# Gated delta rule in a hybrid decoder block: state times keys before the inverse, one application of the inverse

## The chip, the cores and the metric

The kernel runs on one core of one Trainium2 chip. The metric is device time in microseconds (us), the median of several runs. The engines: TensorE (PE in the rows; PEld is its weight load), VectorE (DVE), ScalarE (ACT), GpSimd (POOL) and SyncE (SP), which issues the weight loads.

## What is computed

One decoder block over 16 meta tokens and 256 tokens, width 1024, all in float32: RMS norm, one input projection, differential attention, in parallel a gated delta rule (8 heads of 128), both merged through gates, an output projection, then a mixture of 32 experts. The diff is in the delta rule. The reference computes it in chunks of tokens:

```python
T = triangular_solve(A + eye, eye)                    # the inverse of each chunk
u = einsum('bhnij,bhnje->bhnie', T, v * beta[..., None])
w = einsum('bhnij,bhnjd->bhnid', T, kb * jnp.exp(gc)[..., None])     # kb = k * beta
def step(S, inp):
    v_new = u_n - einsum('bhcd,bhde->bhce', w_n, S)
    o_n = einsum('bhcd,bhde->bhce', qd_n, S) + einsum('bhij,bhje->bhie', qk_n, v_new)
    S = S * gt_n[..., None, None] + einsum('bhcd,bhce->bhde', kd_n, v_new)
    return S, o_n
```

So v_new = T(v·beta) - (T(k·beta·e^gc))S, which is the same as T(v·beta - (k·beta·e^gc)S).

## The kernel before

The kernel takes the meta tokens as a first small chunk and then two chunks (rounds) of 128 tokens, t=0 and t=1. The eight heads are two groups of four, c=0 and c=1, each with eight work buffers `w[0]` to `w[7]` of [128, 4, 128] and three PSUM banks X, Y and Z. The state `S` is [128, 8, 128]. Each round is a chain of named steps, listed in `STEPS`:

- s0 makes the decay matrix and K·K', s1 and s2 turn it and make Q·K'; s3 to s6 build the inverse of 16-wide blocks, x1, t1, x2, t2, x3, t3 join them to 32, 64 and 128 (small 64x64 products). `w[0]` ends as the transposed inverse.
- s7 turns the keys on PE; DVE makes `w[7]` = keys x kdec and `w[2]` = keys x begc (beta·e^gc) from it. POOL masks for x1.
- x3 ends with a small DVE product, t3 with a DVE copy into `w[0]` and `w[4]` = v·beta.
- w multiplies `w[2]` with the inverse, and ACT copies it with scale -1 to `w[6]`.
- v makes v_new in Z from two products per head, `w[0]`·`w[4]` and `w[6]`·S; ACT copies it to `w[5]`.
- o makes the output and the update of S, q the sum of squares for the norm.

A step runs on PE first, then on those of DVE, ACT and POOL that `WORKS` names for it. Semaphores per group and engine (`dn_pe`, `dn_dve`, `dn_act`, `dn_pool`) count the steps; PE's part of a step waits until the other engines have done all earlier steps of its group (`wait_step(..., before=True)`), and the others wait for PE's part of the step. `link` adds a wait for the instruction's own completion, `mark` counts it without the wait.

The order on PE is written out in `MIX_ORDER`. It goes through groups of entries: ten single steps of the meta chunk, then each step of a round for c=0 and c=1. 26 projection tiles (gate2 to gate7, ga0 to ga7, ya0 to ya7, gb0 to gb3) are spread over them by this rule:

```python
while given < len(filler) and given * (len(groups) - 4) < i * len(filler):
    MIX_ORDER.append(("tile", filler[given]))
```

With 18 steps there are 46 groups. PE's order around the rounds comes out as (a step stands for both head groups): [meta s7] [meta w] gate7 [meta m] ga0 [s0] [s1] ga1 [s2] ga2 [s3] [s4] ga3 [s5] [s6] ga4 [s7] ga5 [x1] [t1] ga6 [x2] [t2] ga7 [x3] ya0 [t3] [w] ya1 [v] ya2 [o] [q] ya3 for t=0, and for t=1 [s0] [s1] ya4 [s2] ya5 [s3] [s4] ya6 [s5] ya7 [s6] [s7] gb0 [x1] [t1] gb1 [x2] gb2 [t2] [x3] gb3 [t3] [w] [v] [o] [q]. DVE, ACT and POOL follow `BEHIND`: the same order, except that what they do with a tile's result comes after the next step of c=0. A gate or gb tile is 24 products with operands split in a high and a low part (L740); ACT and DVE split each tile's weights three tiles ahead (L278, L283). A ya tile is eight float32 products (L722).

Lines of the steps: s7 PE L938 to L942, DVE L1733 and L1737, POOL L654; x1, x2 PE L943 (helper L909), ACT L1346; t1 DVE L1740, L1741; x3 PE L951, DVE L1750; t3 PE L954, DVE L1752, L1753; w PE L959 (helper L887), ACT L1348; v PE L967, L968, ACT L1350.

Of the kernel before, what the change touches and what calls it, by code (L numbers as in the profile page):

```python
# [13 lines left out]
P = 128  # L14
D = 1024
NC = D // P
Q = P // 2
# [23 lines left out]
ALU = mybir.AluOpType  # L41
# [23 lines left out]
def hybrid_block(nc, x, meta_tokens, norm1_w, w_in, lambda_q1, lambda_k1, lambda_q2, lambda_k2, da_subln_w,  # L65
# [3 lines left out]
    with ExitStack() as ctx:  # L69
# [278 lines left out]
        TR_NO = {k: i for i, k in enumerate(TR)}  # L348


        STEPS = ["s0", "s1", "s2", "s3", "s4", "s5", "s6", "s7", "x1", "t1", "x2", "t2", "x3", "t3", "w", "v", "o", "q"]
        META_STEPS = ["s0", "s1", "s2", "s3", "s4", "s5", "s6", "s7", "w", "m"]

        DN = [("meta", 0, s) for s in META_STEPS]
        for t in range(TT):
# [2 lines left out]
        WORKS = {  # L358
            "pe": set(STEPS + META_STEPS),
            "dve": {"s0", "s1", "s2", "s3", "s4", "s5", "s6", "s7", "t1", "t2", "x3", "t3", "q", "m"},  # L360
            "act": {"s0", "s2", "s3", "s4", "s5", "s7", "x1", "x2", "w", "v", "o", "q", "m"},
            "pool": {"s1", "s7", "t1", "q"},
        }

# [8 lines left out]
        def works(engine, key):  # L373
            t, _, s = key
            if t == "meta":
                if engine == "pool":
                    return False
                if engine in ("dve", "act") and s == "w":
                    return engine == "dve"
            if engine == "dve" and s == "o":  # L380
                return t == 0
            return s in WORKS[engine]
# [299 lines left out]
        def _(pe):  # L682
# [190 lines left out]
            def dn(t, c, s):  # L873
                w = work[c]
                X, Y, Z = (bank[2 + 3 * c + i][:, :].rearrange("p (h i) -> p h i", h=4) for i in range(3))
                n = 1 if t == "meta" else 4

                for engine in ("act", "dve", "pool"):
                    wait_step(pe, engine, (t, c, s), before=True)
                if (t, c, s) == DN[0]:  # L880
                    pe.wait_ge(tr_copied, len(TR))
                    pe.wait_ge(qk_ready, N_DN)
                    pe.wait_ge(gate_cols, 2)

                def each(o, lhsT, rhs, start=True, stop=True):
                    for h in range(n):
                        last = pe.matmul(o[:, h, :], lhsT(h), rhs(h), start=start, stop=stop)  # L887
                    return last

                if t == "meta":  # L890
                    kT = lambda h: dkT_meta.rearrange("p h i -> p (h i)")
                    vT = lambda h: dvT_meta.rearrange("p h i -> p (h i)")
                    col = lambda h: g[:, 2 * H:2 * H + 1]
                    lower = tri16
                else:
                    cols = slice(META + t * P, META + (t + 1) * P)
                    kT = lambda h: dkT[:, 4 * c + h, cols]
                    qT = lambda h: dqT[:, 4 * c + h, cols]
                    col = lambda h: g[:, t * H + 4 * c + h:t * H + 4 * c + h + 1]
                    lower = tri  # L900
                buf = lambda i: (lambda h: w[i][:, h, :])
                Xs, Ys, Zs = (bank[2 + 3 * c + i][:, 0:4 * Q].rearrange("p (h i) -> p h i", h=4) for i in range(3))

                def both(o, lhsT, rhs, quarters=(0, 1)):

                    for h in range(n):
                        for q in quarters:
                            rows = slice(q * Q, (q + 1) * Q)
                            last = pe.matmul(o[rows, h, :], lhsT[rows, h, :], rhs[rows, h, :], start=True, stop=True,  # L909
                                             tile_position=(q * Q, q * Q))  # L910
                    return last

                T, TT_, X_ = small(c, 6, 0), small(c, 5, 1), small(c, 5, 0)
                if s == "s0":
                    each(X, lambda h: col(h).broadcast_to([P, P]), lambda h: lower)
                    last = each(Y, kT, kT)
                elif s == "s1":
                    for h in range(n):
                        last = pe.transpose(X[:, h, :], w[1][:, h, :], ident)
                    if t != "meta":  # L920
                        last = each(Z, kT, qT)
                elif s == "s2":
                    for h in range(n):
                        last = pe.transpose(Y[:, h, :], w[2][:, h, :], ident)
                elif s == "s3":
                    both(Xs, small(c, 4, 0), small(c, 4, 1))
                    last = both(Zs, small(c, 4, 1), small(c, 4, 0))
                elif s == "s4":
                    both(Ys, small(c, 5, 0), T)
                    both(Xs, small(c, 5, 1), small(c, 5, 0))  # L930
                    last = both(Zs, small(c, 5, 0), small(c, 5, 1))
                elif s == "s5":
                    both(Ys, small(c, 4, 0), T)
                    last = both(Xs, small(c, 4, 1), small(c, 4, 0))
                elif s == "s6":
                    last = both(Zs, small(c, 5, 0), T)
                elif s == "s7":
                    both(Xs, T, ident_c.unsqueeze(1).broadcast_to([P, 4, Q]))  # L938
                    for h in range(n):
                        last = pe.transpose(Y[:, h, :], kT(h), ident)  # L940
                    if t == "meta":
                        last = pe.transpose(Z[:, 0, :], vT(0), ident)  # L942
                elif s in ("x1", "x2"):  # L943
                    last = both(Zs, small(c, 4, 0), T)
                elif s in ("t1", "t2"):
                    both(Xs, X_, TT_)

                    last = both(Zs, TT_, X_, (0, 1) if s == "t1" else (0,))
                elif s == "x3":
                    for h in range(n):  # L950
                        last = pe.matmul(Zs[Q:P, h, :], w[1][0:Q, h, Q:P], T[0:Q, h, :], start=True, stop=True, tile_position=(0, Q))  # L951
                elif s == "t3":
                    for h in range(n):
                        last = pe.matmul(Xs[0:Q, h, :], X_[Q:P, h, :], w[0][Q:P, h, Q:P], start=True, stop=True, tile_position=(Q, 0))  # L954
                elif s == "w":
                    if t == "meta":
                        last = pe.matmul(Z[:, 0, :], w[0][:, 0, :], w[3][:, 0, :], start=True, stop=True)
                    else:
                        last = each(X, buf(2), buf(0))  # L959
                elif s == "m":  # L960

                    for half in range(2):
                        last = pe.matmul(bank[2 + half][:, :], w[7][:, 0, :], um[:, 4 * half:4 * half + 4, :],
                                         start=True, stop=True)
                elif s == "v":
                    for h in range(n):
                        pe.matmul(Z[:, h, :], w[0][:, h, :], w[4][:, h, :], start=True, stop=False)  # L967
                        last = pe.matmul(Z[:, h, :], w[6][:, h, :], S[:, 4 * c + h, :], start=False, stop=True)  # L968
                elif s == "o":
                    for h in range(n):  # L970
                        pe.matmul(Y[:, h, :], S[:, 4 * c + h, :], qT(h), start=True, stop=False)
                        last = pe.matmul(Y[:, h, :], w[5][:, h, :], w[3][:, h, :], start=False, stop=True)
                    if t < TT - 1:
                        last = each(X, buf(7), buf(5))
                elif s == "q":
                    last = pe.matmul(Z, ones, w[6], start=True, stop=True)
                last.then_inc(dn_pe[c], 1)
# [162 lines left out]
        def _(act):  # L1140
# [175 lines left out]
            def dn(t, c, s):  # L1316
# [27 lines left out]
                    last = act.activation(small(c, 5, 1)[:, 0:n, :], Xs[:, 0:n, :], ACT.Copy)  # L1344
                elif s in ("x1", "x2"):
                    last = act.activation(small(c, 5, 0)[:, 0:n, :], Zs[:, 0:n, :], ACT.Copy)  # L1346
                elif s == "w" and t != "meta":
                    last = act.activation(w[6][:, 0:n, :], X[:, 0:n, :], ACT.Copy, scale=-1.0)  # L1348
                elif s == "v":
                    last = act.activation(w[5][:, 0:n, :], Z[:, 0:n, :], ACT.Copy)  # L1350
                elif s == "m":
# [99 lines left out]
        def _(dve):  # L1451
# [233 lines left out]
            def dn(t, c, s):  # L1685
# [46 lines left out]
                elif s == "s7":  # L1732
# [1 line left out]
                    if t == "meta":  # L1734
                        last = tt(b(3), Z, per_head(beta), ALU.mult)
                    else:
                        last = tt(b(2), Y, per_head(begc), ALU.mult)  # L1737
                elif s == "t1":
                    turned = small(c, 5, 1)[:, 0:n, :]
                    tt(turned, Xs, turned, ALU.add)  # L1740
# [6 lines left out]
                        last = tt(diagonal(b(0), q), Xs[rows], small(c, 5, 1)[rows, 0:n, :], ALU.add)  # L1747
                elif s == "x3":

                    last = tt(small(c, 5, 0)[Q:P], Zs[Q:P], per_head(nbeta)[Q:P, :, 0:Q], ALU.mult)  # L1750
                elif s == "t3":
                    dve.tensor_copy(b(0)[0:Q, :, Q:P], Xs[0:Q])  # L1752
                    last = tt(b(4), dv_tok[:, t, hs, :], per_head(beta), ALU.mult)  # L1753
                elif s == "w":

                    last = tt(um, Z[:, 0, :].unsqueeze(1).broadcast_to([P, H, P]),
# [193 lines left out]
```

## Time and profile before

| | |
|---|---|
| median of 3 runs | 745.88 us (745.85 to 747.65) |
| profiled execution | 743.06 us, its span 741.3 us |
| mean granted TensorE clock | 0.943 |
| PE busy | 628.2 us, 85% of the span |
| DVE busy | 322.0 us, 43% |
| ACT busy | 247.1 us, 33% |
| POOL busy | 46.1 us, 6% |
| chain that ended last | PE 67%, DMA 16%, DVE 7%, ACT 4% |

The profile is of one execution. A busy share is the union of an engine's instructions; matmuls are pipelined, so PE's issue times tell more than their ends. The chain of work that ended last follows each step back to what released it. The rounds of the delta rule stand between 264 and 420 us.

### The profile page before, as it was taken

Reading aid. Unit: us, or ns where it says so; the run is one execution under the profiler, and the core shown is the slowest. Engines: PE = TensorE matmul, PEld = TensorE weight load, DVE = VectorE, ACT = ScalarE, POOL = GpSimd, SP = SyncE. Lnnn points to the kernel's source line nnn. Section 1 sums busy time; section 2 is a strip of 40 time slices with the busy share of each in tenths; the row PEclk is TensorE's granted clock in tenths of the full one; section 3 lists DMA queues with packets and bytes.
Section 4 is the critical chain, followed back from the end, with each engine's and each line's share of the span. In section 5 each row is a group of like instructions: output and inputs, shape, how many; then the busy total and the mean of one; then the engine's idle time right before and its main releaser. Section 6 shows DMA issues by size and latency. Waiting matters only on the chain.

```text
span 741.3 us, 12849 instructions
## 1 busy us (share of the span) xinstructions
PE 628.2 (85%) x5127; PEld 498.3 (67%) x5127; DVE 322.0 (43%) x717; ACT 247.1 (33%) x548; POOL 46.1 (6%) x94
## 2 busy tenths in 40 slices
PE   2899999899999979999898999976896686867954
PEld 2899998789988879987788898854333323413321
DVE  4534349899878647522634273143210110201103
ACT  5335547667674434313222550121110110101102
POOL 8000000000000001201111100020000000000000
PEclk9989999999999989999999999997999988978988
DMA  9845443323334411111143077960899999999991
GB/s 292 252 137 167 157 153 114 105 70 112 114 114 132 153 57 59 59 57 57 52 132 104 2 260 262 423 255 1 346 422 422 422 422 422 422 422 423 421 385 57
DMA packets 69686, 156.40 MB, mean 211 GB/s; under 512 B 7042, under 2 KB 56308, under 8 KB 57348
## 3 DMA queue, kind: packets, MB, share of 16 engines
q1 hardware_dynamic: 65792, 154.36, 55.5%
q10 hardware_dynamic: 3844, 1.34, 0.7%
q8 instruction: 35, 0.57, 0.3%
q14 instruction: 15, 0.12, 0.0%
HBM read 154.64 MB, written 1.05 MB: 210 GB/s over the span
## 4 chain that ended last, share of the span: by engine, by line
PE 67%; DMA 16%; DVE 7%; ACT 4%; issue 3%; SPq 1%; POOL 1%; DVEq 0%; ACTq 0%; POOLq 0%
PE bank L740 29%; DMA arena<-in_expert_w_up_dram 15%; PE bank L1069 9%; PE bank L909 4%; PE bank L722 4%; PE bank L729 4%; PE bank L887 2%; PE bank L851 1%; PE bank L828 1%; PE bank L1088 1%; PE bank L1057 1%; SPq L481 1%; PE bank L1095 1%; PE bank L796 1%; DVE w_lo L283 1%
## 5 line engine op out<-in xcount | busy, mean ns | idle before, releaser
L740 PE MATMUL bank<-uT_hi,w_hi 128*128 128x272 f32 (+1 forms) x576 | 175.7, 305 | 5.7 <-issue 4.2
L740 PE MATMUL bank<-uT_lo,w_hi 128*128 128x272 f32 (+1 forms) x576 | 166.7, 289 | 0.0
L740 PE MATMUL bank<-uT_hi,w_lo 128*128 128x272 f32 (+1 forms) x576 | 166.5, 289 | 0.0
L283 DVE TENSOR_TENSOR w_lo<-arena,w_hi 128x1024 fp32r<-128x1024 f32 x80 | 98.6, 1235 | 48.3 <-ACT w_hi L278 48.0
L740 PEld LDWEIGHTS bank<-uT_hi,w_hi 128*128 128x128 f32 x576 | 111.4, 193 | 8.5 <-issue 6.8
L740 PEld LDWEIGHTS bank<-uT_lo,w_hi 128*128 128x128 f32 x576 | 111.5, 194 | 1.5 <-issue 0.5
L740 PEld LDWEIGHTS bank<-uT_hi,w_lo 128*128 128x128 f32 x576 | 111.3, 193 | 0.0
L1069 PE MATMUL bank<-arena 128*32 128x512 f32 x512 | 68.8, 698 | 42.3 <-DMA arena<-in_expert_w_up_dram 39.1
L278 ACT ACTIVATE w_hi<-arena 128x1024 fp32r<-128x1024 f32 x80 | 83.8, 1052 | 4.5 <-PE bank L740 4.2
L1069 PEld LDWEIGHTS bank<-arena 128*32 128x32 f32 x512 | 19.7, 126 | 85.7 <-issue 85.7
L1875 DVE COPY arena<-bank 128x256 f32<-128x256 f32 x8 | 3.4, 425 | 108.6 <-PE bank L1076 108.6
L1423 ACT ACTIVATE arena<-bank 128x256 f32<-128x256 f32 x8 | 3.1, 384 | 120.9 <-PE bank L1069 120.9
L1578 DVE SCALAR_TENSOR_TENSOR arena<-arena 128x272 f32<-128x272 f32 x72 | 37.8, 525 | 7.5 <-ACT arena L1210 5.8
L1088 PE MATMUL bank<-arena 128*32 128x512 f32 x256 | 34.0, 679 | 4.1 <-DVE arena L1882 4.1
L909 PE MATMUL bank<-arena 64*64 64x64 f32 x964 | 34.2, 220 | 1.5 <-ACT arena L1346 0.8
L909 PEld LDWEIGHTS bank<-arena 64*64 64x64 f32 x964 | 31.1, 134 | 5.8 <-issue 1.5
L1057 PEld LDWEIGHTS bank<-arena 128*128 128x128 f32 x256 | 31.1, 199 | 3.3 <-issue 3.3
L1057 PE MATMUL bank<-arena 128*128 128x128 f32 x256 | 31.2, 282 | 0.0
L1095 PE MATMUL bank<-arena 128*128 128x512 f32 x64 | 29.6, 605 | 0.0
L729 PE MATMUL bank<-arena 128*128 128x256 f32 x128 | 28.7, 380 | 1.1 <-DVE arena L1653 1.1
L722 PE MATMUL bank<-arena 128*128 128x256 f32 x128 | 29.3, 382 | 0.0
L729 PEld LDWEIGHTS bank<-arena 128*128 128x128 f32 x128 | 24.0, 190 | 4.3 <-issue 1.2
(319 smaller groups left out, 867.6 us busy)
## 6 DMA issues: line engine op xcount, KB each, us to landing
arena<-in_w_in_dram SPq DMA_DIRECT2D x36, 1024.0 KB, 5.2
arena<-in_expert_w_gate_dram SPq DMA_DIRECT2D x32, 1024.0 KB, 16.7
arena<-in_expert_w_up_dram SPq DMA_DIRECT2D x32, 1024.0 KB, 18.5
arena<-in_expert_w_down_dram SPq DMA_DIRECT2D x32, 1024.0 KB, 17.6
arena<-in_w_branch_attn_dram SPq DMA_DIRECT2D x4, 1024.0 KB, 5.0
arena<-in_w_branch_dn_dram SPq DMA_DIRECT2D x4, 1024.0 KB, 5.2
arena<-in_w_out_dram SPq DMA_DIRECT2D x4, 1024.0 KB, 5.1
arena<-in_x_dram SPq DMA_DIRECT2D x4, 512.0 KB, 5.0
```

The costliest lines, as they stand in the source:

```text
L278: nc.scalar.activation(w_hi[q % NSPLIT], split_source(nc.scalar, q), ACT.Copy).then_inc(w_hi_ready, 1)
L283: nc.vector.tensor_tensor(w_lo[q % NSPLIT], src, w_hi[q % NSPLIT].bitcast(F32), ALU.subtract).then_inc(w_lo_ready, 1)
L722: last = pe.matmul(ps[:, 0:SEQ], unit(u)[:, c, half * P:(half + 1) * P], yaT[:, c, :], start=(c == 0), stop=(c == NC - 1))
L729: last = pe.matmul(ps[:, 0:SEQ], mixT[:, c, t * P:(t + 1) * P], unit(u)[:, c, :], start=(c == 0), stop=(c == NC - 1))
L740: last = pe.matmul(ps[:, 0:b.shape[2]], a[:, c, :], b[:, c, :], start=(c == 0 and i == 0), stop=(c == NC - 1 and i == 2))
L887: last = pe.matmul(o[:, h, :], lhsT(h), rhs(h), start=start, stop=stop)
L909: last = pe.matmul(o[rows, h, :], lhsT[rows, h, :], rhs[rows, h, :], start=True, stop=True, tile_position=(q * Q, q * Q))
L1057: last = pe.matmul(bank[6 + group][:, (c % 4) * P:(c % 4 + 1) * P], u2[:, t, c * P:(c + 1) * P], pick[:, t].rearrange("p e s -> p (e s)"), ...
L1069: last = pe.matmul(bank[4][CAP * e:CAP * (e + 1), :], xg[:, c, CAP * e:CAP * (e + 1)], gate_up(e, odd)[:, c], start=(c == 0), stop=(c == N ...
L1088: last = pe.matmul(bank[6 + half][CAP * e:CAP * (e + 1), :], hidT[:, fc, CAP * e:CAP * (e + 1)], down_of(e)[:, fc, half * 512:(half + 1) * ...
L1095: last = pe.matmul(bank[2 * t + half][:, :], pickT[:, t, :], dsb[:, half * 512:(half + 1) * 512], start=False, stop=False, skip_group_chec ...
L1578: last = stt(a, x_[:, k:k + L], tap(k, c), a, ALU.mult, ALU.add)
```

## The change

The step w leaves the rounds (the meta chunk keeps its own). In s7 PE also multiplies the state onto the keys, K·S, into Z, and DVE scales that by begc into `w[2]`. In x3 DVE makes, behind the small product (which signals at once), v·beta in `w[4]` and `w[4]` - `w[2]` in `w[2]`. v is one product per head, `w[0]`·`w[2]`. With 17 steps the rule above has 44 groups, so the tiles fall elsewhere between the steps: [meta s7] gate7 [meta w] [meta m] ga0 [s0] ga1 [s1] [s2] ga2 [s3] ga3 [s4] [s5] ga4 [s6] ga5 [s7] [x1] ga6 [t1] [x2] ga7 [t2] ya0 [x3] [t3] ya1 [v] ya2 [o] [q] ya3, and for t=1 [s0] ya4 [s1] [s2] ya5 [s3] ya6 [s4] [s5] ya7 [s6] gb0 [s7] [x1] gb1 [t1] gb2 [x2] [t2] gb3 [x3] [t3] [v] [o] [q].

```diff
--- before.py
+++ after.py
@@ -348,7 +348,7 @@
         TR_NO = {k: i for i, k in enumerate(TR)}
 
 
-        STEPS = ["s0", "s1", "s2", "s3", "s4", "s5", "s6", "s7", "x1", "t1", "x2", "t2", "x3", "t3", "w", "v", "o", "q"]
+        STEPS = ["s0", "s1", "s2", "s3", "s4", "s5", "s6", "s7", "x1", "t1", "x2", "t2", "x3", "t3", "v", "o", "q"]
         META_STEPS = ["s0", "s1", "s2", "s3", "s4", "s5", "s6", "s7", "w", "m"]
 
         DN = [("meta", 0, s) for s in META_STEPS]
@@ -358,7 +358,7 @@
         WORKS = {
             "pe": set(STEPS + META_STEPS),
             "dve": {"s0", "s1", "s2", "s3", "s4", "s5", "s6", "s7", "t1", "t2", "x3", "t3", "q", "m"},
-            "act": {"s0", "s2", "s3", "s4", "s5", "s7", "x1", "x2", "w", "v", "o", "q", "m"},
+            "act": {"s0", "s2", "s3", "s4", "s5", "s7", "x1", "x2", "v", "o", "q", "m"},
             "pool": {"s1", "s7", "t1", "q"},
         }
 
@@ -375,8 +375,8 @@
             if t == "meta":
                 if engine == "pool":
                     return False
-                if engine in ("dve", "act") and s == "w":
-                    return engine == "dve"
+                if engine == "dve" and s == "w":
+                    return True
             if engine == "dve" and s == "o":
                 return t == 0
             return s in WORKS[engine]
@@ -940,6 +940,9 @@
                         last = pe.transpose(Y[:, h, :], kT(h), ident)
                     if t == "meta":
                         last = pe.transpose(Z[:, 0, :], vT(0), ident)
+                    else:
+
+                        last = each(Z, kT, lambda h: S[:, 4 * c + h, :])
                 elif s in ("x1", "x2"):
                     last = both(Zs, small(c, 4, 0), T)
                 elif s in ("t1", "t2"):
@@ -953,19 +956,14 @@
                     for h in range(n):
                         last = pe.matmul(Xs[0:Q, h, :], X_[Q:P, h, :], w[0][Q:P, h, Q:P], start=True, stop=True, tile_position=(Q, 0))
                 elif s == "w":
-                    if t == "meta":
-                        last = pe.matmul(Z[:, 0, :], w[0][:, 0, :], w[3][:, 0, :], start=True, stop=True)
-                    else:
-                        last = each(X, buf(2), buf(0))
+                    last = pe.matmul(Z[:, 0, :], w[0][:, 0, :], w[3][:, 0, :], start=True, stop=True)
                 elif s == "m":
 
                     for half in range(2):
                         last = pe.matmul(bank[2 + half][:, :], w[7][:, 0, :], um[:, 4 * half:4 * half + 4, :],
                                          start=True, stop=True)
                 elif s == "v":
-                    for h in range(n):
-                        pe.matmul(Z[:, h, :], w[0][:, h, :], w[4][:, h, :], start=True, stop=False)
-                        last = pe.matmul(Z[:, h, :], w[6][:, h, :], S[:, 4 * c + h, :], start=False, stop=True)
+                    last = each(Z, buf(0), buf(2))
                 elif s == "o":
                     for h in range(n):
                         pe.matmul(Y[:, h, :], S[:, 4 * c + h, :], qT(h), start=True, stop=False)
@@ -1344,8 +1342,6 @@
                     last = act.activation(small(c, 5, 1)[:, 0:n, :], Xs[:, 0:n, :], ACT.Copy)
                 elif s in ("x1", "x2"):
                     last = act.activation(small(c, 5, 0)[:, 0:n, :], Zs[:, 0:n, :], ACT.Copy)
-                elif s == "w" and t != "meta":
-                    last = act.activation(w[6][:, 0:n, :], X[:, 0:n, :], ACT.Copy, scale=-1.0)
                 elif s == "v":
                     last = act.activation(w[5][:, 0:n, :], Z[:, 0:n, :], ACT.Copy)
                 elif s == "m":
@@ -1734,7 +1730,8 @@
                     if t == "meta":
                         last = tt(b(3), Z, per_head(beta), ALU.mult)
                     else:
-                        last = tt(b(2), Y, per_head(begc), ALU.mult)
+
+                        last = tt(b(2), Z, per_head(begc), ALU.mult)
                 elif s == "t1":
                     turned = small(c, 5, 1)[:, 0:n, :]
                     tt(turned, Xs, turned, ALU.add)
@@ -1747,10 +1744,12 @@
                         last = tt(diagonal(b(0), q), Xs[rows], small(c, 5, 1)[rows, 0:n, :], ALU.add)
                 elif s == "x3":
 
-                    last = tt(small(c, 5, 0)[Q:P], Zs[Q:P], per_head(nbeta)[Q:P, :, 0:Q], ALU.mult)
+                    tt(small(c, 5, 0)[Q:P], Zs[Q:P], per_head(nbeta)[Q:P, :, 0:Q], ALU.mult).then_inc(dn_dve[c], 1)
+                    link(tt(b(4), dv_tok[:, t, hs, :], per_head(beta), ALU.mult))
+                    mark(tt(b(2), b(4), b(2), ALU.subtract))
+                    return
                 elif s == "t3":
-                    dve.tensor_copy(b(0)[0:Q, :, Q:P], Xs[0:Q])
-                    last = tt(b(4), dv_tok[:, t, hs, :], per_head(beta), ALU.mult)
+                    last = dve.tensor_copy(b(0)[0:Q, :, Q:P], Xs[0:Q])
                 elif s == "w":
 
                     last = tt(um, Z[:, 0, :].unsqueeze(1).broadcast_to([P, H, P]),
```

## Rows read from the trace of the kernel before

**Rows 1.** The chain that ended last, at the start of the expert stage: start us, us, what

```profile
545.97 18.34 DMA arena<-in_expert_w_up_dram
```

**Rows 2.** Windows: four stretches of the rounds, two stretches of lower clock

```profile
core 0: us, PE busy (x) PEld busy (x) DVE busy (x) ACT busy (x) POOL busy (x), PEclk, DMA share, GB/s
264.27:281.42 17.15, 12.97 (x90) 12.34 (x89) 10.33 (x15) 5.47 (x14) 3.38 (x2) 0.80 0.19 61
270.49:277.31 6.82, 5.44 (x25) 5.17 (x26) 3.14 (x5) 2.71 (x6) 1.28 (x1) 0.50 0.00 0
281.42:332.16 50.74, 49.68 (x731) 46.50 (x730) 25.35 (x52) 14.89 (x31) 4.68 (x4) 1.00 0.18 56
346.87:362.94 16.07, 11.02 (x81) 10.23 (x81) 9.02 (x14) 3.75 (x11) 3.67 (x3) 1.00 0.21 65
362.94:415.12 52.18, 49.26 (x699) 45.16 (x698) 22.09 (x47) 13.96 (x28) 4.85 (x4) 0.97 0.31 102
403.60:407.02 3.42, 3.42 (x18) 3.42 (x17) 1.23 (x2) 0.00 (x0) 0.00 (x0) 0.50 0.00 0
```

**Rows 3.** Waits of PE, 242 to 428 us: total us, times, longest

```profile
PE bank L919 <- issue: 5.1, 2, 2.7
PE bank L919 <- DVE arena L1709: 3.8, 2, 2.4
```

**Rows 4.** Timeline of PE around v at t=0: start us, us, what

```profile
328.59 0.38 PE L967 MATMUL bank<-arena 128*128 128x128 f32 x2
332.16 0.38 PE L722 MATMUL bank<-arena 128*128 128x256 f32 x1
```

**Rows 5.** Timeline of x3, t3 and w at t=0

```profile
316.97 0.43 DVE L1750 TENSOR_TENSOR arena<-bank,arena 64x256 f32<-64x256 f32 x1 [0.91 <-PE bank L951]
...
321.69 0.42 DVE L1752 COPY arena<-bank 64x256 f32<-64x256 f32 x1 [3.51 <-PE bank L954]
322.12 0.69 DVE L1753 TENSOR_TENSOR arena<-arena 128x512 f32<-128x512 f32 x1
...
322.92 2.38 PE L887 MATMUL bank<-arena 128*128 128x128 f32 x16 [0.80 <-issue]
```

**Rows 6.** Timeline of the meta chunk's w and m

```profile
256.58 0.46 PE L957 MATMUL bank<-arena 128*128 128x128 f32 x2 [0.21 <-DVE arena L1735]
...
257.84 1.22 DVE L1756 TENSOR_TENSOR arena<-bank,arena 128x1024 f32<-128x1024 f32 x1
...
259.72 1.88 PE L963 MATMUL bank<-arena 128*128 128x512 f32 x4
```

**Rows 7.** Timeline: s1 of group 1 at t=0; a table load at t=1

```profile
274.50 1.09 PE L919 MATMUL bank<-arena 128*128 128x128 f32 x4 [1.38 <-DVE arena L1709]
...
388.24 1.28 ACT L1217 ACT_TABLE_LOAD   x1
```

**Rows 8.** Timeline behind s7 at t=0

```profile
299.91 0.69 DVE L1733 TENSOR_TENSOR arena<-bank,arena 128x512 f32<-128x512 f32 x1 [2.68 <-PE bank L940]
300.52 0.68 DVE L1737 TENSOR_TENSOR arena<-bank,arena 128x512 f32<-128x512 f32 x1
301.37 0.74 POOL L654 TENSOR_TENSOR arena<-arena 128x256 f32<-128x256 f32 x1 [20.47 <-DVE arena L1737]
302.57 1.23 DVE L283 TENSOR_TENSOR w_lo<-arena,w_hi 128x1024 fp32r<-128x1024 f32 x1
302.76 1.62 POOL L654 TENSOR_TENSOR arena<-arena 128x256 f32<-128x256 f32 x1 [0.65 <-DVE arena L1737]
```

**Rows 9.** Windows: s3-s4, s7, x2-t2 at t=0; x1-t1, t2-x3 at t=1

```profile
284.45:289.26 4.81, 4.81 (x161) 4.74 (x160) 2.73 (x6) 1.43 (x4) 0.00 (x0) 1.00 0.54 171
298.60:300.82 2.22, 2.22 (x41) 1.92 (x41) 0.91 (x2) 0.66 (x2) 0.00 (x0) 1.00 0.94 306
310.05:313.22 3.17, 3.15 (x82) 2.95 (x81) 1.11 (x4) 1.88 (x4) 0.00 (x0) 1.00 0.03 8
387.11:391.32 4.21, 3.38 (x97) 3.07 (x96) 0.96 (x3) 3.27 (x5) 0.78 (x2) 1.00 0.93 303
398.48:403.07 4.59, 3.30 (x66) 3.01 (x65) 2.98 (x8) 1.33 (x2) 0.00 (x0) 1.00 0.67 228
```

## The prediction, made before the changed kernel was run

> **What bounds the kernel now.** I looked first at the page's busy shares and its chain of work that ended last, to see who sets the pace (TensorE, PE in the rows), then at the stage of the delta rule, 255 to 420 us, the only one that the diff touches. What leaves that stage comes out at the end: behind it the chain runs on PE through the projections and the router into the first expert batch, and only from 546 us does it stand on expert weights, whose loads are issued once a batch of experts has used its slots [rows 1]. So a microsecond won or lost before 420 us moves the end by about one.
>
> Inside the stage I measured four stretches by windows: round t=0 from s0 to the end of s2, then to the end of v; the same for t=1 [rows 2]. In the long ones PE is busy for 49.68 of 50.74 and 49.26 of 52.18 us: mostly the tiles and products themselves set the pace. In the short ones it is busy for 12.97 of 17.15 and 11.02 of 16.07 us, and the waits say why: s1 waits for VectorE's (DVE) masked decay, 5.1 and 3.8 us over four waits [rows 3]. The granted clock stands at 0.50 from 270.49 to 277.31 and from 403.60 to 407.02 us, and at 1.00 elsewhere in the stage [rows 2].
>
> **Part 1, work on PE.** One 128x128x128 product costs 0.223 us: v issues 16 of them from 328.59 to 332.16 [rows 4]. The four products of w per head group become the four of K·S in s7, an even trade. v falls from eight to four per group: 16 fewer in all, 16 x 0.223 = 3.6 us off PE, 1.8 a round.
>
> **Part 2, the step w goes.** At t=0, t3's second half has issued by 322.05, and w starts at 322.92, behind the DVE copy and the product with beta [rows 5]; its second half waits again. The wait of some 0.8 us and the second of 0.25 go: 1.1; at t=1 0.9 by the same reading. ScalarE's copy with scale -1 goes too, hidden now behind ya1 at t=0 and the other group at t=1, so worth nothing.
>
> **Part 3, DVE work that moves.** x3 now has the small product, v·beta and the subtraction, 0.69 us for each large one (the subtraction is priced as the product, both 128x512 from SBUF) [rows 5]. t3 needs only the first, but DVE takes its queue in order: group 1's small product stands behind group 0's two large ones and a tile's output.
>
> **Part 4, the order written out for PE.** This is the part that speaks against the change. With 17 steps the 26 tiles fall between other pairs of steps. Worked out by the formula of the order, the new neighbours without a tile between are w-m (start), then at t=0 s1-s2, s4-s5, s7-x1, t1-x2, x3-t3, and at t=1 s1-s2, s4-s5, s7-x1, x2-t2, x3-t3-v. No longer neighbours are s0-s1, s3-s4, s5-s6 (s6-s7 at t=1), x1-t1, t3-w, and x2-t2 at t=0, t2-x3 at t=1. The costs, each followed through the queues:
>
> *w-m at the start.* m waits for DVE's 1.22 us spread of w's result; gate7 covered it, w at 256.58 and m at 259.72 [rows 6]. Without the cover w to m takes about 1.7 us instead of 0.2, and the 0.2 to 0.5 us that w itself waits is now covered: +1.1.
>
> *s0 to s2.* s1's second half can't start before DVE's decay of group 1, 274.4 at t=0 [rows 7], with ga1 before it or not. Behind it remain s1 (1.35 us at full clock), DVE's two products and GpSimd's q product (POOL, 1.3), now with no tile over them, while the tile's 2.9 us fill the first wait. t=0: 17.15 to 16.1, -1.1. t=1: 16.07 to 15.3, -0.8.
>
> *s7-x1.* s7 takes 2.22 us for both groups now, 1.1 to 1.2 each [rows 9], and 0.89 more per group for K·S: 2.1. x1 waits for POOL's product, which waits for both DVE products of s7. From s7's start: group 0's DVE 2.2 to 3.5, POOL to 4.4 (0.74 alone), x1 at 4.55 where PE was free at 4.2; group 1's PE part ends at 4.2, DVE 4.35 to 5.6, POOL to 6.5, x1 at 6.7 where PE was free at 5.1. Idle 0.35 + 1.6 = 1.95 us at t=0; at t=1 ScalarE's table load of 1.28 us [rows 7] falls between its two copies and holds gb0's output on DVE before group 1: 2.35. Before, a tile stood there and covered all of it.
>
> *t1-x2 at t=0.* DVE 0.75 for two 128x256 operations, POOL 0.74 [rows 8] and three handovers of 0.15 make 1.9 us, against 0.96 for the other group's t1: idle 1.0 + 0.45.
>
> *x3-t3.* The first small product ends 1.15 us after x3's start [rows 5]. v·beta, the subtraction and the tile's output then fill DVE to 2.7, group 1's small product to 3.15; t3's second half starts at 3.25 where PE was free at 1.8: 1.6 with the first gap, in each round. At t=1 v follows at once, and waits until the t3 copy at 4.85 where PE was free at 3.8: 1.1.
>
> The waits that go are read from pairs of steps that had no tile between: a 64x64 product costs 0.060 us (80 in 4.81) [rows 9], so x2-t2 at t=0, 40 of them, waited 3.17 - 2.4 = 0.8 us; x1-t1 at t=1, 48, waited 4.21 - 2.9 = 1.3; t2-x3 at t=1, 24 and eight of 0.13, 4.59 - 2.5 = 2.1 [rows 9]. For s5-s6, s6-s7 and x1-t1 at t=0 I estimate 0.3 each in the same way.
>
> Sums at full clock. t=0, ga2 to v: 50.74 - 1.8 (work) - 2.5 (w 1.1, x1-t1 0.3, x2-t2 0.8, s5-s6 0.3) + 5.15 (1.95, 1.45, 1.6, s4-s5 0.15) + 0.4 (more tiles start behind small products, 3.65 against 3.46 for a ya tile) = 52.0, **+1.3**. t=1, ya5 to v: 52.18 - 1.8 - 4.6 (w 0.9, x1-t1 1.3, t2-x3 2.1, s6-s7 0.3) - 1.7 (gb3 takes 4.55 us at clock 0.50, others 2.85) + 6.0 (2.35, x2-t2 0.8, 1.6, 1.1, s4-s5 0.15) + 0.2 = 50.3, **-1.9**. With the start +1.1 and the two short stretches -1.9 the whole is **-1.4 us**: the 3.6 us of saved work and 2 us around w are mostly spent on new waits.
>
> **The clock.** That sum has no stretch at 0.50. Before there are two: one came behind a 2.4 us wait, the other behind short gaps amid the small products of t2 and x3; yet s0-s1 at t=1, with as long waits, kept 1.00 [rows 2, 3]. The first cost about 1.1 (s1's second half in 2.45 instead of 1.35), the second 1.7. The new order has more places of that kind (s7-x1 twice, x3-t3 twice, s1-s2 twice), but a fall that meets an idle PE costs little. I take two falls at 1.1: +2.2. Bounds: none, 0; four, +4.4. Sum -1.4 + 2.2 = **+0.8**. The profiled execution took 743.06 (span 741.3), the median of the three runs is 745.88; I put the difference on the median: **746.7**.
>
> The Trainium skill ("TensorE: Matmul & The Clock Gate", HAM oscillation) says that gaps in the matmul stream bring the array back to half rate and that the next products start cold. The trace agrees at 270.49 and not at t=1, as above; by that rule alone each of the six new gaps would count, which is the second rival.
>
> POOL's product took 0.74 us alone and 1.62 us beside DVE's split at 302.57 [rows 8]; I price it at 0.74 in s7-x1, since the next split there waits for ScalarE, behind x1's copies. If it were 1.62 there, +0.9 a round. The Trainium skill ("SBUF — State Buffer") calls the pair of ports an exclusive lock; the row agrees: POOL ends 0.58 us after the split.
>
> **The rivals.** *The waits don't come, PE's saved work does.* If s7-x1 costs nothing (POOL's and DVE's work for group 1 done in time), 4.3 us less: 742.4. For it: PE is over 95% busy in the long stretches, so these steps have mostly been covered. Against: s7 signals once, at its end, and 2.5 us of DVE, POOL and handovers stand between it and x1 of the same group. It decides from 3 us less waiting than I count. Chance 0.26.
>
> *The clock falls at most of the new gaps.* One mechanism: PE's activity thins around s7-x1 and x3-t3, the clock goes to 0.50, and tiles or v and o behind it run at half rate, 1.7 us as gb3 did. With four falls at about 1.3 us: -1.4 + 5.2 = +3.8, 749.7; slower by over 0.3% from the third full one. For it: the fall at 403.60 came after gaps of under 1 us. Against: t=1 s0-s1. Chance 0.26.
>
> The forecast, gaps and savings about even, has 0.48, with its own range 744.2 to 748.1.
>
> **How the numbers follow.** 0.3% is 2.2 us, about what a measurement of this kernel tells from no change. Faster is the first rival (0.25, the rest of it within), slower the second (0.27 with a little of the forecast's edge), same 0.48. The range reaches into both: 742.0 (two falls fewer, or most of s7-x1 hidden) to 749.5 (four falls).
>
> **What would show it.** x1 behind s7 waiting for POOL, about 2 us in each round; t3's second half waiting for DVE's small product by 1.5 us; m behind DVE's spread; v in 1.8 us for both groups; s0-s1 without its first wait; stretches at 0.50, where and how many. It would be wrong if s7-x1 shows under 1 us of waits, or if the projections and the first expert batch don't shift along with the stage.

## The result and the profile after

The changed kernel takes 752.25 us (median of four, 751.39 to 754.74) against 745.87 before: ratio 1.0113, interval [1.0065, 1.0161]. It is slower by about 1.1%. Forecast was 746.7, no change, in a range up to 749.5. The profiled execution took 751.41 us (span 749.6, 8.3 more than before), mean granted clock 0.934.

First the windows of the kernel after: the four stretches of [rows 2] (s0 to s2 and ga2 to v at t=0, s0 to s2 and ya5 to v at t=1), then every stretch of the stage at clock 0.50.

```profile
core 0: us, PE busy (x) PEld busy (x) DVE busy (x) ACT busy (x) POOL busy (x), PEclk, DMA share, GB/s
264.43:280.59 16.16, 11.37 (x90) 10.57 (x89) 10.53 (x18) 5.76 (x15) 2.56 (x2) 0.86 0.20 65
280.59:336.49 55.90, 51.24 (x715) 47.31 (x713) 25.95 (x51) 13.74 (x27) 2.90 (x4) 0.95 0.14 40
351.20:366.50 15.30, 11.21 (x81) 10.21 (x81) 9.21 (x15) 4.27 (x12) 3.64 (x3) 1.00 0.22 70
366.50:420.52 54.02, 49.28 (x682) 45.13 (x681) 23.34 (x49) 12.34 (x24) 3.75 (x4) 0.93 0.31 99
275.93:282.75 6.82, 4.35 (x21) 3.72 (x20) 6.31 (x13) 2.49 (x5) 2.56 (x2) 0.50 0.00 0
330.54:333.95 3.41, 3.41 (x10) 2.70 (x9) 0.47 (x2) 0.00 (x0) 0.00 (x0) 0.50 0.00 0
395.39:398.80 3.41, 3.41 (x27) 3.29 (x28) 0.91 (x1) 1.33 (x2) 0.00 (x0) 0.50 0.04 11
415.87:422.70 6.83, 5.72 (x27) 5.75 (x28) 1.30 (x3) 1.20 (x2) 0.00 (x0) 0.50 0.01 2
```

The short stretches shrank, from 17.15 and 16.07 to 16.16 and 15.30 us. The long ones grew, from 50.74 and 52.18 to 55.90 and 54.02, though PE has 32 records fewer on the page (5095 against 5127). And the stage has four falls of the clock where [rows 2] has two, two of them (6.8 us) twice as long as the others. The rest of the 8.3 us: +1.2 from the meta chunk's w and m, -1.0 ahead of it, 1.05 in o and q at t=1 (the last third of that last fall lies there), and 1.8 behind the stage.

The waits of PE, 242 to 428 us (total, times, longest), and what stands behind s7 at t=0:

```profile
PE bank L924 <- POOL arena L651: 4.8, 4, 2.1
PE bank L909 <- POOL arena L654: 4.8, 6, 1.6
PE bank L957 <- issue: 3.2, 2, 1.7
PE bank L919 <- DVE arena L1705: 2.3, 1, 2.3
PE bank L919 <- issue: 1.8, 1, 1.8
PE bank L963 <- DVE arena L1755: 1.4, 1, 1.4
PE bank L887 <- issue: 1.3, 1, 1.3
```

```profile
306.07 0.69 DVE L1729 TENSOR_TENSOR arena<-bank,arena 128x512 f32<-128x512 f32 x1 [0.60 <-PE bank L887]
306.31 0.68 PE L909 MATMUL bank<-arena 64*64 64x64 f32 x16 [0.28 <-POOL arena L654]
306.68 0.68 DVE L1734 TENSOR_TENSOR arena<-bank,arena 128x512 f32<-128x512 f32 x1
...
307.53 0.72 POOL L654 TENSOR_TENSOR arena<-arena 128x256 f32<-128x256 f32 x1 [1.37 <-DVE arena L1734]
308.40 0.68 PE L909 MATMUL bank<-arena 64*64 64x64 f32 x16 [1.41 <-POOL arena L654]
```

x1 of both groups waits for GpSimd's product, which waits for both of VectorE's; in [rows 8] a tile lay over the same chain. Next, x3 and t3 at t=0:

```profile
325.99 0.43 DVE L1747 TENSOR_TENSOR arena<-bank,arena 64x256 f32<-64x256 f32 x1 [2.45 <-PE bank L954]
326.45 0.69 DVE L1748 TENSOR_TENSOR arena<-arena 128x512 f32<-128x512 f32 x1
...
327.17 0.69 DVE L1749 TENSOR_TENSOR arena<-arena 128x512 f32<-128x512 f32 x1
327.90 0.42 DVE L1646 TENSOR_TENSOR arena<-bank,arena 128x256 f32<-128x256 f32 x1
328.35 0.43 DVE L1747 TENSOR_TENSOR arena<-bank,arena 64x256 f32<-64x256 f32 x1
...
328.88 0.65 PE L957 MATMUL bank<-arena 64*64 64x64 f32 x8 [1.72 <-issue]
```

The reader sees DVE's queue in its order: group 0's small product, v·beta (L1748), the subtraction (L1749), a tile's output, and only then group 1's small product, for which t3's second half has waited 1.72 us. And t2 of both groups, which stands by itself between two tiles here, takes 2.01 us from its first product to the tile behind it:

```profile
319.62 2.08 PE L909 MATMUL bank<-arena 64*64 64x64 f32 x48
321.63 3.72 PE L722 MATMUL bank<-arena 128*128 128x256 f32 x16
```

Behind the stage the shift passes on whole: from the first product of gb4 to the first of the expert stage it is 86.88 us in both profiles (420.10 to 506.98, and 426.55 to 513.43). Then the first gather runs 6.01 us instead of 4.87, at the lower clock, and the chain reaches the weights 1.2 us later still:

```profile
513.43 6.01 PE bank L1055 x32
...
553.65 18.24 DMA arena<-in_expert_w_up_dram
```

### The profile page after: what moved, and what is told of

Same layout as the page of the kernel before. It is cut to its first block, busy times and chain, and to the rows that moved or that the text cites. A ratio compares the mean times of both kernels' runs of the same rounds, so it can differ in the third digit from the quotient of the medians.

```text
span 749.6 us, 12781 instructions
## 1 busy us (share of the span) xinstructions
PE 629.5 (84%) x5095; PEld 499.8 (67%) x5095; DVE 325.0 (43%) x721; ACT 245.0 (33%) x544; POOL 45.8 (6%) x94
## 3 DMA queue, kind: packets, MB, share of 16 engines
HBM read 154.64 MB, written 1.05 MB: 208 GB/s over the span
## 4 chain that ended last, share of the span: by engine, by line
PE 66%; DMA 16%; DVE 8%; ACT 4%; issue 4%; SPq 1%; POOL 1%; DVEq 0%; POOLq 0%; ACTq 0%
PE bank L740 29%; DMA arena<-in_expert_w_up_dram 15%; PE bank L1067 9%; PE bank L909 4%; PE bank L729 4%; PE bank L722 4%; PE bank L887 2%; PE bank L851 2%; PE bank L828 1%; PE bank L1055 1%; PE bank L1086 1%; SPq L481 1%; PE bank L1093 1%; DVE w_lo L283 1%; PE bank L796 1%
## 5 line engine op out<-in xcount | busy, mean ns | idle before, releaser
L1055 PEld LDWEIGHTS bank<-arena 128*128 128x128 f32 x256 | 32.2, 205 | 3.3 <-issue 3.3
L722 PE MATMUL bank<-arena 128*128 128x256 f32 x128 | 31.0, 398 | 0.0
L729 PE MATMUL bank<-arena 128*128 128x256 f32 x128 | 28.7, 380 | 1.1 <-DVE arena L1649 1.1
L722 PEld LDWEIGHTS bank<-arena 128*128 128x128 f32 x128 | 24.9, 199 | 4.1 <-issue 0.5
```

Source lines behind the costliest of these rows:

```text
L722: last = pe.matmul(ps[:, 0:SEQ], unit(u)[:, c, half * P:(half + 1) * P], yaT[:, c, :], start=(c == 0), stop=(c == NC - 1))
L729: last = pe.matmul(ps[:, 0:SEQ], mixT[:, c, t * P:(t + 1) * P], unit(u)[:, c, :], start=(c == 0), stop=(c == NC - 1))
L1055: last = pe.matmul(bank[6 + group][:, (c % 4) * P:(c % 4 + 1) * P], u2[:, t, c * P:(c + 1) * P], pick[:, t].rearrange("p e s -> p (e s)"), ...
```

## The experiments

My theory after the result: the algebra itself saves time, the places that the tiles got cost more than it saves, partly in waits and partly in falls of the clock that follow them. The rival: the algebra costs, through K·S in s7 and the longer DVE part of x3.

**The changed kernel again.** 

> The changed kernel again, unaltered, with more executions: how far its time scatters and how that goes with the granted clock. Expected: median 751 to 753, executions over 5 us apart, the slower ones at the lower mean clock.

Measured: 753.02 us (750.46 to 753.27, six executions), ratio 1.0094 [1.0058, 1.0131]. The scatter is under 3 us, less than I expected, and the slower ones don't show the lower mean clock (752.69 at 0.925, 753.23 at 0.936). Its profile (span 751.5) repeats the first one: the same four stretches to 0.06 us and the same four falls, all some 0.4 us later. The kernel before scatters more: of 23 further executions of it, those at a mean clock of 0.943 to 0.945 took 740.0 to 743.2 us, those at 0.933 took 742.2 to 748.0.

**Old places, new algebra.**

`spots` counts the missing w of each round again, so that each tile falls between the same steps as in the kernel before.

```diff
+        spots = [i + (i >= 24) + (i >= 41) for i in range(len(groups))]
...
-            while given < len(filler) and given * (len(groups) - 4) < i * len(filler):
+            while given < len(filler) and given * 42 < spots[i] * len(filler):
```

> The changed algebra (17 steps) with all 26 tiles between the same steps as before. Theory (the loss is where the tiles fall, and the clock behind the new gaps): s7-x1, t1-x2 and x3-t3 have a tile between again; 3.6 us of PE work and the waits of w are gone; span 5 to 6 us under that of before, about 736, median about 740. Rival (the algebra itself costs: K times S in s7 and the longer DVE part of x3 sit on the path): still over before, about 750.

Measured: 734.12 us (733.52 to 739.47), ratio 0.9843 [0.9804, 0.9882]. Its windows, the same four stretches and then its falls:

```profile
263.49:280.66 17.17, 12.40 (x91) 11.84 (x89) 10.35 (x15) 5.01 (x13) 3.40 (x2) 0.80 0.19 61
280.66:328.40 47.74, 47.60 (x715) 44.64 (x714) 27.55 (x54) 14.05 (x30) 3.79 (x4) 1.00 0.16 47
343.12:359.20 16.08, 12.28 (x82) 11.39 (x81) 9.02 (x14) 3.76 (x11) 3.66 (x3) 0.89 0.21 66
359.20:410.23 51.03, 48.70 (x683) 44.64 (x681) 24.26 (x49) 12.77 (x26) 3.78 (x4) 0.93 0.32 105
270.78:277.61 6.83, 4.45 (x23) 4.18 (x22) 3.64 (x6) 2.29 (x6) 1.28 (x1) 0.50 0.00 0
349.29:352.70 3.41, 2.76 (x12) 2.47 (x12) 1.50 (x3) 1.76 (x5) 0.00 (x0) 0.50 0.00 0
400.49:407.32 6.83, 6.79 (x35) 6.48 (x36) 4.61 (x7) 0.26 (x1) 0.00 (x0) 0.50 0.05 15
```

The short stretches are those of before to 0.02 us. The long one at t=0 is 3.0 us shorter than before and PE is busy for 47.60 of 47.74 us: 1.8 us of products and 1.1 us of waits around w are gone, and nothing has taken their place. The rival falls: with the tiles in their old places the algebra is a gain of about 11 us by the medians. This profile was one of its two slowest executions (739.42), so its span shows less.

**New places, old algebra.**

Here `spots` leaves w out of the count, and no tile may fall ahead of w.

```diff
+        spots = [i - (i > 24) - (i > 42) for i in range(len(groups))]
...
-            while given < len(filler) and given * (len(groups) - 4) < i * len(filler):
+            while given < len(filler) and given * 40 < spots[i] * len(filler) and i not in (24, 42):
```

> The algebra of before (18 steps) with the tiles between the steps where the changed kernel has them, w directly behind t3. Theory (placement): slower than before by about as much as the change, +5 to +9 us, since 3.6 us of products stay and w's waits too, but DVE's queue at x3 is short. Rival (algebra): within 2 us of before.

Measured: 748.39 us (746.30 to 753.15), ratio 1.0047 [1.0018, 1.0077]; the profiled execution, at 750.52, one of the slower. By the medians that is 3 us slower, less than expected:

```profile
263.74:279.90 16.16, 11.66 (x90) 10.86 (x89) 10.53 (x18) 5.76 (x15) 2.56 (x2) 0.85 0.19 65
279.90:336.67 56.77, 52.84 (x731) 49.29 (x730) 24.38 (x49) 14.93 (x29) 2.90 (x4) 0.95 0.16 50
351.38:366.69 15.31, 11.21 (x82) 10.22 (x82) 9.21 (x15) 4.28 (x12) 3.64 (x3) 1.00 0.22 68
366.69:421.39 54.70, 51.14 (x699) 46.46 (x697) 21.95 (x47) 13.43 (x26) 3.74 (x4) 0.94 0.30 98
```

The short stretches are those of the changed kernel to 0.01 us. The long ones are 6.0 and 2.5 us over before, and there are four falls too, at 274.93 (6.8 us), 326.13, 367.09 and 397.81 (3.4 us each). So in this profile the places cost the old algebra 6.8 us of the stage, and the stage is as long as in the changed kernel (162.63 us from s0 to gb4, against 162.12): what the new algebra saves is lost again. By the medians the places cost the old algebra 3 us and the new one 18. The waits show one thing that the new algebra adds here. The new x3 puts 1.4 us more per group in DVE's queue just where these places leave x3 and t3 side by side, and t3 waits 3.2 us in all, against 0.3 with the old algebra. What else sets the medians apart, one profile of each doesn't say.

**Gaps filled.** Products of `ident` and `tri` that nothing reads, into a PSUM bank that is free at that time.

```diff
+                def keep_busy(k):
+                    for i in range(k):
+                        pe.matmul(bank[3][:, (i % 4) * P:(i % 4 + 1) * P], ident, tri, start=True, stop=True)
...
+                if t != "meta":
+                    keep_busy({("s1", 0): 9, ("s1", 1): 8, ("x1", 0): 6, ("x3", 1): 0, ("t3", 0): 7}.get((s, c), 0))
+                    if t == 1 and (s, c) == ("t3", 1):
+                        keep_busy(4)
```

> The changed kernel with extra products into a free PSUM bank in the gaps behind s1, x1 and t3 (nothing reads them; 9, 8, 6, 7 and 4 products of 0.22 us, a little less than each gap). Theory (falls of the clock cost some 6 us of the 8): no stretch at 0.50 between 270 and 425 us, span about 743 to 745. Rival (the gaps themselves cost it, the clock little): span 749 to 751 or more, whatever the clock shows.

Measured: 745.63 us (743.11 to 746.31), ratio 1.0002 [0.9973, 1.0030]. The order and the queues are those of the changed kernel, with work added, and 6.6 us are gone:

```profile
264.53:280.34 15.81, 14.23 (x124) 13.70 (x123) 10.18 (x17) 5.76 (x15) 2.57 (x2) 1.00 0.20 66
280.34:333.65 53.31, 51.77 (x741) 48.18 (x740) 26.30 (x52) 13.75 (x27) 2.91 (x4) 1.00 0.14 42
348.37:363.70 15.33, 14.62 (x116) 13.95 (x115) 9.22 (x15) 4.27 (x12) 3.66 (x3) 1.00 0.22 69
363.70:414.60 50.90, 50.41 (x717) 46.09 (x715) 23.35 (x49) 12.35 (x24) 3.76 (x4) 1.00 0.32 105
```

The clock stays at 1.00 in all four, and against the changed kernel they are 0.35, 2.6, 0 and 3.1 us shorter, 6.0 in sum; o and q at t=1 are back at 4.98 from 6.03. That is what its falls cost in the stage: 7.1 us for 20.5 us at 0.50.

**The same in the kernel before** (9 products behind s0, 9 behind s1 of group 0, 3 in x3 at t=1). 

> The kernel before with extra products that nothing reads in its gaps behind s0, s1 and x3 (9, 9 and 3 of 0.22 us). Theory (its two falls of the clock cost it 1.1 and 1.7 us in the profile): none left in the stage, 2 to 4 us under before. Rival (only the changed kernel suffers from falls): within 1 us, or slower by the added products.

Measured: 742.20 us (739.80 to 744.57), ratio 0.9965 [0.9939, 0.9992], no fall in the stage. So the kernel before paid some 3 us for its own (3.0 by the medians, 2.6 by the ratio, 2.8 in the stage of the profiles).

**The same with the old places and the new algebra.** 

> The changed algebra, tiles where before has them, and the extra products of the last experiment. Theory (waits and clock add up): no fall in the stage, the best so far, 1 to 4 us under the version without the extra products, some 730 to 733. Rival: within 1 us of it.

Measured: 736.04 us (733.63 to 737.46), ratio 0.9898 [0.9860, 0.9936], no fall in the profiled stage. It is not better than 734.12 without the extra products, though its filling stands where that of the kernel before does. The likely reason is that there is little to gain: six of the eight executions without filling ran at a mean clock of 0.947 to 0.951, and 0.951 is what a profile of nearly the same kernel without any fall in the stage shows (the last experiment). The profile above is of a slow execution, so this is not shown.

The three filled kernels have no fall in the stage and so give the terms at full clock. The stage from s0 at t=0 to gb4, in before, before filled, changed filled, and old places with the new algebra filled:

```profile
264.27:420.10 155.83, 142.22 (x1714) 130.28 (x1713) 70.86 (x138) 46.05 (x94) 17.99 (x14) 0.97 0.21 69
264.48:417.55 153.07, 147.12 (x1792) 135.17 (x1791) 70.83 (x138) 46.04 (x94) 17.99 (x14) 1.00 0.22 70
264.53:419.58 155.05, 150.33 (x1810) 137.97 (x1809) 73.13 (x142) 44.13 (x90) 14.32 (x14) 1.00 0.22 69
264.33:412.27 147.94, 143.09 (x1760) 131.56 (x1759) 74.48 (x142) 43.56 (x90) 17.06 (x14) 1.00 0.23 72
```

The algebra in the same places saves 5.1 us (153.07 to 147.94). The new places cost 7.1 us in waits (147.94 to 155.05), and the changed kernel's falls another 7.1 (155.05 to 162.12). The fillings differ and each figure is from one profile, so they are rough.

**The subtraction out of x3.** DVE scales K·S by e^gc alone in s7, then, ahead of its part of x1, subtracts it from v and multiplies the difference by beta, which gives the same `w[2]`. x3 keeps only the small product.

```diff
-                        last = tt(b(2), Z, per_head(begc), ALU.mult)
+                        last = tt(b(2), Z, per_head(egc), ALU.mult)
...
+                if s == "x1":
+                    k, hs, b2 = t * H + 4 * c, slice(4 * c, 4 * c + 4), work[c][2]
+                    wait_step(dve, "dve", (t, c, "s7"))
+                    link(tt(b2, dv_tok[:, t, hs, :], b2, ALU.subtract))
+                    mark(tt(b2, b2, beta[:, k:k + 4].unsqueeze(2).broadcast_to([P, 4, P]), ALU.mult))
```

> The changed kernel with the subtraction out of x3: DVE scales K times S by e^gc in s7, and right behind s7 subtracts it from v and multiplies by beta, so x3 on DVE is the small product alone. Theory (DVE's queue at x3 holds t3): t3's second half no longer waits (3 us over both rounds) and v at t=1 follows at once (1.2), and the clock falls behind t3 go too: 4 to 8 us under the changed kernel, span 742 to 746. Rival (x3's DVE work is hidden, or the two products now hold POOL and x1 by as much): within 2 us of the changed kernel.

Measured: 743.35 us (742.16 to 746.56), ratio 0.9981 [0.9955, 1.0006]: 8.9 us under the changed kernel, somewhat more than the 4 to 8 expected. The stretch at t=1, from ya5 to v, is the one to read:

```profile
363.88:413.87 49.99, 47.54 (x683) 43.44 (x681) 23.74 (x49) 12.33 (x24) 4.04 (x4) 0.97 0.33 107
```

54.02 us have become 49.99, at a mean clock of 0.97 instead of 0.93. The waits of x1 and x2 for GpSimd rose from 4.8 to 5.3 us in all, so the rival's part (the moved products hold GpSimd) is there, at half a microsecond.

**A tile between x3 and t3** (ya0 and gb3, by leaving groups 22 and 39 out of the rule). 

> The changed kernel with the other tile moved: ya0 and gb3 stand between x3 and t3 instead of between t2 and x3. Theory (DVE's queue in x3 holds t3's second half, 1.7 us in each round, and v at t=1 by 1.3): these waits go, t2-x3 waits under 1 us in their place, and the fall behind t3 may go: 3 to 7 us under the changed kernel, as taking the subtraction out of x3 did. Rival (DVE's longer part costs in any order): within 1 us.

Measured: 745.19 us (744.37 to 751.36), ratio 1.0023 [0.9993, 1.0054]: 7.1 us under the changed kernel, at the upper end of the 3 to 7 expected. The two waits of t3, 3.2 us, are gone; t2-x3 waits 2.3 us in their place, more than the 1 us expected. The stage has three falls of 3.4 us instead of four with two of 6.8.

**A tile between s7 and x1** (groups 17 and 34). 

> The changed kernel with one tile a round moved: ga5 and gb0 stand between s7 and x1 instead of between s6 and s7. Theory (x1 behind s7 waits for DVE and GpSimd, 1.9 and 2.9 us, and the clock falls there at t=1): x1 waits under 0.3 us, 4 to 6 us under the changed kernel. Rival (the tile only changes place and the wait comes back at s6-s7): within 1 us of it.

Measured: 747.96 us (745.17 to 749.61), ratio 1.0054 [1.0031, 1.0077]: 4.3 us under the changed kernel. The waits for L654 fell from 4.8 to 1.2 us; those of x1 are gone, and what is left is that of x2 at t=0. There are still four falls, three of 3.4 us and one of 6.8.

**Both waits taken away.** 

> The changed kernel with the subtraction right behind s7 and ga5 and gb0 between s7 and x1: both of the two largest new waits taken away, the other new neighbours left. Theory (waits add up): 9 to 13 us under the changed kernel, 739 to 743. Rival (what one takes away the other had already): no better than the better of the two alone, 743.

Measured: 737.68 us (735.73 to 738.73), ratio 0.9890 [0.9854, 0.9926]: 14.6 us under the changed kernel, a little more than 8.9 and 4.3 make together (13.2), and more than the 9 to 13 expected. The stage has two falls of 3.4 us.

**Old places and the subtraction out of x3.** 

> The changed algebra with the tiles where before has them and the subtraction right behind s7. Theory (with a tile between x3 and t3 DVE's long part of x3 is hidden already): within 1.5 us of the version with the subtraction in x3. Rival (DVE's queue at x3 matters in any order): 3 us under it.

Measured: 734.53 us (733.78 to 736.97), ratio 0.9887 [0.9850, 0.9923], the same as with the subtraction in x3. With a tile between x3 and t3 DVE's longer queue costs nothing. Its profile (span 732.0, clock 0.951) shows the waits of s1 as before and above, and no fall in the stage:

```profile
PE bank L920 <- issue: 5.1, 2, 2.7
PE bank L920 <- DVE arena L1711: 5.0, 2, 2.6
```

## Why the prediction was wrong, by its own steps

**The step that failed** is "I take two falls at 1.1: +2.2. Bounds: none, 0; four, +4.4." There are four, and they cost 7.1 us in the stage (the changed kernel against the same with its gaps filled), 1.8 each: even my bound for four was too low. What was missed is how many come and how long they last. I priced them without a length. Two last 3.4 us and two 6.8, 20.5 us at 0.50 in all, which at 7.1 us is 0.35 for each microsecond. In the two short ones, from 330.54 to 333.95 and 395.39 to 398.80, PE is busy for every microsecond, so a tile behind a gap pays the full 1.7 us, as gb3 did before. The first long one meets a PE that is busy for 4.35 of its 6.82 us, the last one covers v and the start of o (5.72 of 6.83). By the stretches I estimate 1.2 us for the first and 2.5 for the last, taking 1.7 for each short one. The second rival had the mechanism and its sign (four falls, 749.7), at 1.3 each.

In the profiles the forecast was a span of 742.1 us (741.3 + 0.8), and 749.6 was measured, 7.5 more: 4.9 from the falls (7.1 against 2.2), 1.8 from the sum at full clock, 1.8 behind the stage, and -1.0 ahead of it. By the medians the range's upper end was missed by 2.75 us.

**The sum at full clock** was -1.4. The filled kernel gives its measure: against before its stretches are -1.3, +2.6, -0.7 and -1.3, with the start's +1.2 together +0.4. The stretches were forecast at 16.1, 52.0, 15.3 and 50.3 and are 15.8, 53.3, 15.3 and 50.9. Most of what was missing: t2 takes 2.0 us, not 1.45 (its last four products per group go to one quarter of the array and take the 0.13 us of x3's, where I had 0.06). So two of the waits that I let go were largely work that stays: x2-t2 at t=0 with 0.8 us, where [rows 9] has PE busy for 3.15 of 3.17 us, and t2-x3 at t=1 with 2.1, where the trace of before has waits of 1.3 in x3. That is some 0.55 us in each round. And x3-t3 waits 1.7, not 1.6, twice.

**Right**: the new waits, by place and size. x1 behind s7 0.3 and 1.4 us at t=0 against 0.35 and 1.6, and 1.9 in all at t=1 against 2.35; x2 behind t1 at t=0 1.2 against 1.45; GpSimd's product 0.73 and 0.72 us there, the price of one that runs alone; t3 1.7 against 1.6; v at t=1 1.25 against 1.1; m 1.4; s0 to s2 shorter by 1.0 and 0.8 against 1.1 and 0.8. Right too that v falls to 1.8 us (334.70 to 336.49), that the copy with scale -1 was worth nothing, and that what leaves the stage comes out at the end. What I didn't count is the 1.8 us behind the stage, where the first expert batch met more of the lower clock. They don't go with the change: from gb4 to the end it is 321.2 us in the profile of before, the shortest of all, 323.0 and 324.5 in the two profiles of the changed kernel, and 325.3 in that of before with its gaps filled.

**The first rival** (the waits don't come, the saved work does) is what the algebra does once the tiles stand in their old places: 734.1 us, more than the 742.4 I gave it. At full clock its gain in the stage is 5.1 us (the filled kernels), near the 3.6 of products and 2 of waits around w. Some 3 us more are the falls of the kernel before, which most executions with the old places and the new algebra seem to be without (0.947 to 0.951 in six of eight, against 0.929 to 0.947). About 3 of the 11 us stay open. Its argument that PE is over 95% busy in the long stretches holds at t=0 only; at t=1 it is 94% (49.26 of 52.18).

**The Trainium skill** ("TensorE: Matmul & The Clock Gate", HAM oscillation) names the mechanism: a wait of PE brings the array back to half rate, and the next products start cold. The traces agree with that in the four falls. But the section speaks of longer waits than any here, of which the longest in the changed kernel is 2.3 us, so my reading that by its rule each of the six new gaps would count went beyond it. That four falls come, the runs show and not the page. I set t=1's s0-s1 against the rival, which kept 1.00 through 5 us of waits; one quiet place is weak evidence. With the old places and the new algebra nearly the same waits had a fall at 349.29 with the subtraction in x3 and none with it moved.

## What to carry to other kernels

When a step is taken out of a chain whose order a rule spreads filler over, work out the new neighbours before anything else: here the algebra is worth 1.6% in the old places, and the shift of its covers cost more than all of it, half in waits and half in falls of the clock. Give a product that one group's next step needs its place ahead of the long work of the other group, or put a tile over it. And price a gap on TensorE at its own length plus a fall that may land on the work behind it, some 1.8 us here, before calling it small.

## What the runs showed of the hardware

Adding 30 products at t=0 and 34 at t=1 that nothing reads made the changed kernel 6.6 us faster, because the clock stayed up; the same in the kernel before gave about 3 us, and in the fastest version nothing. Short waits are enough: before the fall at 403.60 in the kernel before, PE had waited 0.4 and 0.9 us between small products. Whether a given gap brings a fall isn't settled by its length: the two kernels with the old places and the new algebra have nearly the same waits (s1 8.6 and 10.1 us in all, the longest 2.4 and 2.7), and show three falls in one profile (span 737.7) and none in the other, with the subtraction moved (span 732.0). The same program profiled twice had the same four falls. A 64x64 product costs 0.06 us when the products alternate between two quarters of the array and 0.13 us when they all go to one (t2, x3 and t3). The kernel before scatters over 739.35 to 749.19 us in 29 executions on one chip, which is more than its first three runs (745.85 to 747.65) let one expect, and goes with the mean clock: 747.3 us and more at 0.929, 740.5 and less at 0.945 and above; comparisons of it under 1% need a dozen executions of each.
